# A transformer encoder on one core: the low half of each weight tile by an adding DMA instead of a POOL subtraction

## The reference, cut to what matters

```python
x = layer_norm(x, ln0_g, ln0_b)
for i in range(DEPTH):                                   # DEPTH = 2
    mix = hybrid_mixer(x, w_in[i], ..., w_out[i], ...)
    x = layer_norm(ALPHA * x + mix, ln1_g[i], ln1_b[i])
    ffn = conv_glu(x, w_up[i], conv_w[i], conv_b[i], w_down[i])   # D_FF = 2816
    gate = jax.nn.sigmoid(x @ w_ple_gate[i] + b_ple_gate[i])
    ple = p[i].astype(x.dtype) @ w_ple[i]
    x = layer_norm(ALPHA * x + ffn + gate * ple, ln2_g[i], ln2_b[i])

# conv_glu: g, v = split(x @ w_up); g = a 3-tap convolution of g along the tokens, plus conv_b
#           return (gelu(g) * v) @ w_down
```

## Time and profile before

| | us |
|---|---|
| median of three executions | 1299.53 |
| the profiled execution, first to last instruction | 1299.6 |
| PE busy | 1269.0 (98%) |
| DVE busy | 582.0 (45%) |
| POOL busy | 539.2 (41%), of it 467.3 in 192 subtractions L502 |
| ACT busy | 486.8 (37%), of it 201.5 in 192 copies L590 |
| DMA, mean busy share of the 16 engines | 29% |

### The profile page before, as it was taken

The page is one execution under the profiler, slowest core; times in us unless marked ns, Lnnn a source line. Parts: engine busy times, 40 slices in busy tenths (PEclk is TensorE's granted clock), DMA queues, the critical chain, the costliest instruction groups (busy, mean ns, idle before and its releaser), DMA issues.

```text
span 1299.6 us, 17927 instructions
## 1 busy us (share of the span) xinstructions
PE 1269.0 (98%) x6152; PEld 1041.6 (80%) x6152; DVE 582.0 (45%) x864; ACT 486.8 (37%) x855; POOL 539.2 (41%) x276
## 2 busy tenths in 40 slices
PE   7999999999999999999999999999999999999996
PEld 6777778888888888888877777788888888888885
DVE  7876565753222224211388666557322222341108
ACT  3445444324433333322143545432343333333221
POOL 6532113446544444344365213144564444434443
PEclk9999899999999999999999999999999999999999
DMA  6321012244333333232232202033343323322231
GB/s 206 98 66 50 28 55 82 65 130 130 114 100 95 96 97 98 79 98 97 69 87 78 66 17 82 17 131 97 97 131 112 97 85 108 99 81 97 97 97 65
DMA packets 121317, 116.72 MB, mean 90 GB/s; under 512 B 4769, under 2 KB 95905, under 8 KB 121249
## 3 DMA queue, kind: packets, MB, share of 16 engines
q1 hardware_dynamic: 121248, 115.85, 29.0%
HBM read 113.74 MB, written 2.10 MB: 89 GB/s over the span
## 4 chain that ended last, share of the span: by engine, by line
issue 39%; PE 27%; POOL 26%; DVE 4%; DVEq 2%; POOLq 1%; DMA 1%; ACT 0%; SPq 0%; ACTq 0%
POOL w_lo L502 24%; PE ps L1189 5%; PE ps L1191 4%; PE ps L1190 4%; PE ps L1361 4%; PE ps L1332 3%; PE ps L1347 2%; PE ps L1330 2%; POOL ln_r L508 1%; DVE hbuf L911 1%; PE ps L1337 1%; PE ps L1372 1%; DMA scratch<-in_ln_b_dram 1%; PE ps L1312 1%; POOLq L501 1%
## 5 line engine op out<-in xcount | busy, mean ns | idle before, releaser
L502 POOL TENSOR_TENSOR w_lo<-raw,w_hi 128x1024 fp32r<-128x1024 f32 x192 | 467.3, 2438 | 574.2 <-ACT w_hi L590 574.2
L1189 PE MATMUL ps<-xt_hi,w_hi 128*128 128x512 f32 x704 | 273.9, 389 | 0.0
L1190 PE MATMUL ps<-xt_lo,w_hi 128*128 128x512 f32 x704 | 273.9, 389 | 0.0
L1191 PE MATMUL ps<-xt_hi,w_lo 128*128 128x512 f32 x704 | 273.9, 389 | 0.0
L590 ACT ACTIVATE w_hi<-raw 128x1024 fp32r<-128x1024 f32 x192 | 201.5, 1054 | 126.2 <-PE ps L1191 60.2
L1189 PE MATMUL ps<-w_hi,stat 128*128 128x512 f32 x480 | 190.8, 398 | 0.0
L1191 PE MATMUL ps<-w_hi,stat 128*128 128x512 f32 x480 | 187.6, 391 | 0.0
L1190 PE MATMUL ps<-w_lo,stat 128*128 128x512 f32 x480 | 187.3, 390 | 0.0
L1189 PEld LDWEIGHTS ps<-xt_hi,w_hi 128*128 128x128 f32 x704 | 132.1, 188 | 27.8 <-issue 0.2
L1191 PEld LDWEIGHTS ps<-xt_hi,w_lo 128*128 128x128 f32 x704 | 132.1, 188 | 27.3
L1190 PEld LDWEIGHTS ps<-xt_lo,w_hi 128*128 128x128 f32 x704 | 132.1, 188 | 27.3
(11 more groups left out here) (120 smaller groups left out, 1426.9 us busy)
## 6 DMA issues: line engine op xcount, KB each, us to landing
raw<-in_w_up_dram SPq DMA_DIRECT2D x88, 512.0 KB, 3.8
raw<-in_w_down_dram SPq DMA_DIRECT2D x44, 512.0 KB, 3.3
raw<-in_w_in_dram SPq DMA_DIRECT2D x26, 512.0 KB, 3.8
raw<-in_w_out_dram SPq DMA_DIRECT2D x16, 512.0 KB, 3.8
raw<-in_w_ple_gate_dram SPq DMA_DIRECT2D x16, 512.0 KB, 4.1
scratch<-in_ln_g_dram SPq DMA_DIRECT2D x5, 512.0 KB, 4.6
scratch<-in_ln_b_dram SPq DMA_DIRECT2D x5, 512.0 KB, 6.3
raw<-in_w_ple_dram SPq DMA_DIRECT2D x4, 512.0 KB, 3.7
```

The lines of the kernel that those rows point to most:

```text
L502: pool.tensor_tensor(w_lo[:, n, :], raw[:, n % RAW, :], w_hi[:, n, :].bitcast(F32), ALU.subtract).then_inc(w_split.sem, 1)
L1189: pe.matmul(out, a[0], b[0], start=first, stop=False)
L1190: pe.matmul(out, a[0], b[1], start=False, stop=False)
L1191: return pe.matmul(out, a[1], b[0], start=False, stop=last)
```

## The change

ACT now makes two copies of each raw tile: the high half to `w_hi` as before, and the same with scale -1 to `w_lo`. POOL, instead of subtracting, issues a DMA that reads `raw` and adds it onto `w_lo` in place (SBUF to SBUF, 512 KB read from `raw`, with `accum_op=add` on the float32 view of `w_lo`). The sum is the same low half. That it is made is now told by the landing of the DMA (`lo_landed`, one semaphore for each of the 8 buffers) instead of the end of a POOL instruction (`w_split`). SP waits for that landing before it loads into the raw buffer again, and PE before it uses the slot. Two loops of SP are unrolled further so that each wait names its own semaphore. There is one more instruction per slot on ACT and one short semaphore instruction on POOL.

```diff
             def lo(n, value):
 
                 pool.wait_ge(w_hi_done.sem, value)
-                pool.tensor_tensor(w_lo[:, n, :], raw[:, n % RAW, :], w_hi[:, n, :].bitcast(F32),
-                                   ALU.subtract).then_inc(w_split.sem, 1)
+                pool.sem_inc(lo_begun.sem, 1)
+                pool.dma_start(w_lo[:, n, :].bitcast(F32), raw[:, n % RAW, :], accum_op=ALU.add).then_inc(lo_landed[n].sem, 16)
...
             def first_lo(s):
                 pool.wait_ge(w_hi_done.sem, s + 1)
-                pool.tensor_tensor(w_lo[:, s, :], first_raw(s), w_hi[:, s, :].bitcast(F32), ALU.subtract).then_inc(w_split.sem, 1)
+                pool.dma_start(w_lo[:, s, :].bitcast(F32), first_raw(s), accum_op=ALU.add).then_inc(lo_landed[s].sem, 16)
...
                 act.wait_ge(raw_landed[n % RAW].sem, landed)
                 act.wait_ge(w_used.sem, used)
-                act.activation(w_hi[:, n, :], raw[:, n % RAW, :], ACT.Copy).then_inc(w_hi_done.sem, 1)
+                act.activation(w_hi[:, n, :], raw[:, n % RAW, :], ACT.Copy)
+                act.activation(w_lo[:, n, :], raw[:, n % RAW, :], ACT.Copy, scale=-1.0).then_inc(w_hi_done.sem, 1)
...
+        def wait_lo(eng, layer, s, rounds=0):
+
+            landed = lo_landed[s % SLOTS]
+            eng.wait_ge(landed.sem, landed.at(layer, 16 * (s // SLOTS + 1)) + rounds * 16)
...
                 def raw_free(s):
-                    sp.wait_ge(w_split.sem, w_split.at(layer, s - AHEAD - RAW + 1))
+                    wait_lo(sp, layer, s - RAW)
...
                 def split(s):
-                    pe.wait_ge(w_split.sem, w_split.at(layer, s - AHEAD + 1))
+                    wait_lo(pe, layer, s)
```

More of the change, by code:

```diff
@@ L210, in encoder @@
         w_hi_done = sig("w_hi_done", STREAM, AHEAD)
-        w_split = sig("w_split", STREAM, AHEAD)
+        lo_landed = [sig(f"lo_landed{n}", 16 * STREAM // SLOTS) for n in range(SLOTS)]
+        lo_begun = sig("lo_begun", STREAM)
         w_used = sig("w_used", STREAM, SLOTS)
@@ L447, in _ @@
                 sp.dma_start(ln_b, bcast(ln2_b[bass.ds(layer, 1)].rearrange("a n -> (a n)"))).then_inc(norm_landed.sem, 16)
[L448 to L451, removed]
+                with sp.Fori(0, FT // 4) as i:
+                    for v in range(8):
+                        wait_lo(sp, layer, UP_AT + v - RAW, i)
+                        load(UP_AT + v, up_source(layer, i * 4 + v // 2, v % 2), 8)
+                for v in range(8 * (FT // 4), 2 * FT):
+                    raw_free(UP_AT + v)
+                    load(UP_AT + v, up_source(layer, v // 2, v % 2), 8)
                 raw_free(DOWN_AT)
                 load(DOWN_AT, down_source(layer, LOOPED), 1)
-                with sp.Fori(0, LOOPED // 2) as i:
-                    for v in range(2):
+                with sp.Fori(0, LOOPED // 8) as i:
+                    for v in range(8):
                         s = DOWN_AT + 1 + v
-                        sp.wait_ge(w_split.sem, w_split.at(layer, s - AHEAD - RAW + 1) + i * 2)
-                        load(s, down_source(layer, i * 2 + v), 1)
+                        wait_lo(sp, layer, s - RAW, i)
+                        load(s, down_source(layer, i * 8 + v), 1)
                 for r in range(1, REST):
@@ L601, in first_hi @@
                 act.wait_ge(landed.sem, 16)
-                act.activation(w_hi[:, s, :], first_raw(s), ACT.Copy).then_inc(w_hi_done.sem, 1)
+                act.activation(w_hi[:, s, :], first_raw(s), ACT.Copy)
+                act.activation(w_lo[:, s, :], first_raw(s), ACT.Copy, scale=-1.0).then_inc(w_hi_done.sem, 1)
             first_hi(0)
@@ L1443, in _, with up_tile @@
                             signal(ins, gate_full, q == 3, t)
-                def up_tile(bank, s, n):
+                def up_tile(bank, s, n, i=0):
                     pe.wait_ge(h_done.sem, h_done.at(layer, -1) + n)
                     for v in range(2):
-                        pe.wait_ge(w_split.sem, w_split.at(layer, s[0] + v - AHEAD + 1) + s[1])
-                        a = slot(s[0] + v, KD)
+                        wait_lo(pe, layer, s + v, i)
+                        a = slot(s + v, KD)
                         for k in range(KD):
@@ L1459, in _ @@
                     for v in range(4):
-                        up_tile(2 * (v % 2), (UP_AT + 2 * v, i * 8), i * 4 + v)
+                        up_tile(2 * (v % 2), UP_AT + 2 * v, i * 4 + v, i)
                 for j in range(LOOPED, FT):
-                    up_tile(2 * (j % 2), (UP_AT + 2 * j, 0), j)
+                    up_tile(2 * (j % 2), UP_AT + 2 * j, j)
                 def down(j, s, t, first, last, halves=(0, 1)):
@@ L1482, in _ @@
                         pe.wait_ge(h_split.sem, h_split.at(layer, v + 1) + i * 8)
-                        pe.wait_ge(w_split.sem, w_split.at(layer, s - AHEAD + 1) + i * 8)
+                        wait_lo(pe, layer, s, i)
                         for t in range(TT):
```

## The result

The changed kernel takes 1447.47 us (median, 1446.13 to 1448.39) against 1298.22 us (1296.70 to 1301.92) of the kernel before: the ratio is 1.114, with a 95% interval from 1.112 to 1.117. It is **slower by 149 us**. The forecast was 1413, with a range from 1315 to 1545. The profiled execution spans 1446.0 us, at a granted clock of 0.962 of the full level (before: 0.992).

A forecast was written before the change was run, and what follows sets the result against it. PE was taken as the bound, busy 1269.0 of 1299.6 us, and the longer weight stream as stopping it. Losses of 54.7 us a layer, 109.4 for two, plus 4 at the start gave 1299.6 + 113.4 = 1413 us, range 1315 to 1545.

The forecast's parts named there:

- The cycle: One raw buffer's copies, add and next load: from 7.7 to 12.3 us, against PE's 10.88 per pair of slots.
- X: Time from the end of ACT's second copy to the adding DMA's landing: between 3.3 and 8.1 us, taken as 6.0.
- Start: PE's wait for the third slot at the start grows by about X + 1.05 - 2.4, taken as 4 us.
- Gate stage: Slots 26 and 28, each layer: `norm_hi` comes at 270.1 instead of 265.06; of the 5.0 us, 3 charged.
- Up stage: Per layer: +16.6 us for four cycles at the entry, then +25.2 for 18 cycles over slots 38 to 74.
- Down stage: Slots 74 to 96 of each layer: 11 cycles, each 0.9 us over PE's pace, +9.9 us.
- I cost it at nothing there: Attention stage: ACT's second copy, 1.05 us per slot, is covered by ACT's idle time and costs nothing.
- rival E: Feed-forward stage: PE's idling brings slow clock stretches, 2 us left at every third cycle, +38 us, 1451; chance 0.05.
- A: The add is quick, X = 4.4, so only entry, gate and start lose: 1326 us; chance 0.20.
- B: The DMA engines become the bound, a slot taking 6.8 us instead of 5.44: 1515 us; chance 0.20.
- C: Faster: X under 1.35 us, the cycle no longer than now and DVE free of POOL: 1292 us; chance 0.03.
- D: DVE holds up POOL's descriptors, 0.69 us for each add in 33 cycles per layer: +46 us, 1459; chance 0.05.

The follow-up runs named there:

- e5: The changed kernel without ACT's second copy in the layers, the DMA adding onto whatever `w_lo` holds: 1365.14 us, ratio 1.053.
- e6: The changed kernel with ACT's two copies in the other order, so the add starts beside the high-half copy: 1383.38 us, ratio 1.064.
- e9: The changed kernel with each raw buffer handled as two halves of 512 columns, each loaded, copied, added and released by itself: 1335.95 us, ratio 1.029.
- e8: The changed kernel with the adding DMA only in slots 24 to 95 of each layer, POOL's subtraction and one ACT copy elsewhere: 1433.40 us, ratio 1.103.
- e1: The kernel before with ACT's second copy alone, POOL's subtraction then overwriting it as before: 1317.57 us, ratio 1.014.
- e3: The changed kernel with a DMA that copies `raw` to `w_lo` instead of adding it: 1320.75 us, ratio 1.017.
- e4: The changed kernel with the adding DMA over only the first 512 of 1024 columns of each slot: 1323.12 us, ratio 1.020.

## Why the prediction was right, and where it was off

**The mechanism was right.** The cycle was forecast as 12.3 us and most cycles are 12.2 to 12.3 (the exceptions are below); PE idles at the entry, released by DVE's product (16.6 forecast, 18.56 measured), and in most tiles behind it. e5, e6 and e9 shorten this cycle, all with the same bytes moved by the DMAs, and give back 82, 64 and 111 us.

**The terms of the cycle were each off, and cancelled.** X was taken as 6.0 and is 5.3 (0.6 until POOL begins, 4.7 to the landing; the median landing of all adds is 5.1). The load was kept at 3.8 "landing little later": beside the adds it takes 4.9 in that cycle, 4.4 in the median. The copies were right (2.1, and 2.0). The right sum is partly luck.

**Term by term** (forecast, then measured):

- Start: 4, and 2.7.
- Gate stage: 3 of the 5.0 us of delay were charged. It costs 6 to 7 (+6.8 and +6.3 in e8, whose attention stages have the same slow stretch as before's, in layer 1 alone). `norm_hi` came at 272.82, which is the 270.1 worked out plus the 2.7 of the start. PE then waited 6.56 us where it had waited 0.71, and ran on at a PEclk of 0.52 (the window from 275 to 280). The products said to lie ahead hid nothing.
- **Up stage: 16.6 + 25.2 = 41.8, and 50.9.** The step that failed is "18 cycles, each 12.3 - 10.9 = 1.4": it leaves out ACT's table loads. They make two cycles in eight longer, and the mean cycle is 12.7 instead of 12.3; that is 8 us a layer (below, The long cycles). The entry took 50.6 us where 49.2 was forecast.
- Down stage: 9.9, and 9.8 in layer 1. The cycle is 11.9 (11.4 to 13.2) for 11.8 forecast. In layer 2 the down stage and the end come to 6.0; what the other 3.9 went to I did not follow.
- **The other step that failed: "I cost it at nothing there", stretched over all slots below 24.** That was said of the second copy in the attention stage, and e1 bears that out. But I gave X no price there either, and the input product lies in the same stretch of slots: PE goes through its slots faster than the attention stage does, and waits for the landing of the adds, or for work behind a late copy on ACT. In layer 2 this costs 5.2 us more of waits (7.7 for 2.5), and layer 1 has the same pattern. I had read one row of ACT and none of the input product.
- Ahead of the up stage of layer 2, +19.2 stood against a forecast of 3: 6.3 the gate, 5.2 these waits, and 7.8 the slow stretch at 850 to 870, which no add caused as far as the rows show, since the same wait of 0.90 stands ahead of it before. In layer 1 it is the other way round: +6.9 contains the 5 us that before loses at the earlier trace rows and after doesn't.

**The long cycles.** Between slots 38 and 74 of layer 1 the first copies of a pair lie 12.1 to 12.5 us apart except for five, which are 13.8 to 14.0. One of the five (534.22) has a load that landed in 6.3 us. The other four stand behind table loads. Once in four tiles ACT loads a table of functions, 1.28 us, ahead of the middle tap, and once more ahead of the gelu. The kernel before has them too (346.39 and 350.46), but there its PE never waits in the up stage. ACT in the kernel after, then PE, then the add and the load issued between 399 and 402 us with their landing:

```profile
393.20 1.06 ACT L599 ACTIVATE w_hi<-raw 128x1024 fp32r<-128x1024 f32 x1 [5.79 <-DMA raw<-in_w_up_dram]
394.17 1.04 ACT L600 ACTIVATE w_lo<-raw 128x1024 fp32r<-128x1024 f32 x1
395.23 1.28 ACT L717 ACT_TABLE_LOAD   x1
397.06 1.04 ACT L599 ACTIVATE w_hi<-raw 128x1024 fp32r<-128x1024 f32 x1
407.09 1.06 ACT L599 ACTIVATE w_hi<-raw 128x1024 fp32r<-128x1024 f32 x1 [7.37 <-DMA raw<-in_w_up_dram]
...
398.00 0.75 PE L1200 MATMUL ps<-xt_hi,w_hi 128*128 128x512 f32 x1 [2.45 <-DVE hbuf L1075]
...
w_lo<-raw POOLq DMA_DIRECT2D x1, 512.0 KB, 5.7
raw<-in_w_up_dram SPq DMA_DIRECT2D x1, 512.0 KB, 6.4
```

The gelu starts 1.3 us late, so PE waits 2.45 us instead of about 1.1, and ACT's next copy (397.06) comes 13.7 us after the one two slots before (383.33). The add of that slot is issued at 399.62, close ahead of the next load at 400.52. That load lands in 6.4 us instead of 4.7, and the copy at 407.09 closes a cycle of 13.9. (That the add beside it holds the load up is my reading; it is so at all four.) The same follows the table loads at 344.31, 445.8 and 496.3, and those of layer 2.

**So rival E is not what happened**, though its size (every third cycle, 2 us) is close to this one (every fourth tile, two cycles of 1.4 to 1.7); that is luck. The clock falls at 398, when the gelu and the copy are already late. In layer 2 the wait of 2.35 us at 1108.95 is followed by no slow stretch, and the cycles there are 13.3 and 13.9 all the same (1108.01, 1118.06). A slow stretch eats later waits, as the prediction had said: each of the 20 tiles from the entry on starts on PE within 0.7 us of the end of DVE's product, those behind a slow stretch too (410.63 for 410.40).

The sum: the up stages miss by 2 x 9.1, layer 2's front by 16.2, layer 1's by 3.9, less 1.3 at the start and 4.0 down: 33.0, and 113.4 + 33.0 = 146.4, the growth of the span.

**The rivals.** A (X = 4.4) would have been near 1326; e3, where the plain copy makes X 4.5 (second copy over at 403.2, SP goes on at 407.7), measures 1321, so A's arithmetic holds and its premise doesn't. The estimate from the Trainium skill that stood beside it ("DMA: Bandwidth & Descriptors", the anatomy of a DMA on the gpsimd path: 2.0 us plus bytes over 436 GB/s) was low: the copy alone, with one source, took 3.7 where that formula gives 3.2, and the add 5.1 where the estimate was 4.4. The rule of the Trainium skill, "Collectives: The Full Stack", section on the fold count, that an adding DMA is slower because it reads two sources, is in keeping with the factor 2.2 in engine time; no run here tells reading from adding. B is refuted by e9, and its premise was too high: it charged the engines 4.9 us for an add and 1.88 for a load, 6.8 per slot; they are busy for 2.92 and 1.7, 4.6 of each 5.44. C would have needed X under 1.35. D did not happen: POOL's issue takes 859 ns in the feed-forward stage, 868 in the mean of all and 1186 at most, where D wanted 690 more in each. E is answered above; its 58 cycles of 1.4 us were 36 of 1.4 and 22 of 0.9 by the prediction's own terms.

**A formula that came out of the runs.** For a mean cycle Z the up stage loses 4 Z - 32.6 + 18 (Z - 10.9), the second part not below 0. With the means of layer 1 from slot 38 to 74, table loads included, it gives for after (342.29 to 570.98, 12.7) 50.6 where 50.9 was measured, for e6 (336.40 to 548.83, 11.8) 30.8 for 30.2, and for e5 (333.87 to 539.01, 11.4) 22.0 for 22. With the undisturbed cycles of 12.3, 11.25 and 11.25 it falls short, by 9 us for after.

## What to carry to other kernels

A buffer that is loaded, used and loaded again has a cycle, and each operation that reads it lies in that cycle at its full latency, not at its share of an engine. Taking work off a half-idle engine into a DMA puts the landing time of the DMA into the chain: here 2.4 us of POOL became 5.3. Before such an edit, add up the cycle, compare it with the pace of the consumer, and look at every stage where buffers fill anew (entries, changes of stage), since here they had no slack where the steady state had some. When the cover goes, look also at what it had hidden: a table load of 1.28 us in every fourth tile cost nothing before and about 8 us a layer after. If the cycle is too long and memory is full, cut the buffer in halves that are released one by one: in e9 this gave back three quarters of the loss.

## What had not been expected of the hardware

- An adding DMA within SBUF keeps the DMA engines busy 2.2 times as long as a copy of the same 512 KB (2.92 against 1.34 us), and POOL issues it in 868 ns instead of 536, for half the bytes too (e4: 868).
- Loads of `w_up` land in 4.4 us in the median beside the adds, 3.9 beside plain copies, 3.8 before.
- Beside the adds most loads of `w_up` land in 3.7 to 4.9 us, and 12 of the 88 in 6.2 to 6.8. A load issued 2.4 us behind an add (363.7) took 4.7, one 0.9 us behind (400.52) 6.4 and one 2.1 us behind (527.8) 6.3; what divides them is not shown.
- ACT's table loads, 1.28 us each, stand in the loop of the feed-forward stage, two of them once in four tiles; there are 19 in all in each of the two kernels.
- The clock. In layer 1 of after's up stage PE waits 1.1 to 1.2 us (372.04, 384.38, 422.79) and the clock stays up; it waits 2.4 us at 398.00 and 448.56 and it goes down. In layer 2, 2.35 us at 1108.95 and it stays up. The same wait of 0.90 us in the attention stage is followed by a slow stretch in one layer and not in the other. PE is busy for 38.8 us more in all; in the up stages none of it can be seen to lengthen the time, since PE waits there for the stream.
- A DMA share of 0.98 over 120 us did not hold PE up at all in e9.
